# Attention scores as two full products and one split short one, and second-half copies on ScalarE in every unit

## The reference

```
sc = einsum('bhqd,bhkd->bhqk', q_blk, k).astype(float32) * scale
p  = softmax(sc, axis=-1)
o  = einsum('bhqk,bhkd->bhqd', p, v)
```

## Time and profile before

| what | us |
| --- | --- |
| median of 3 runs | 2406.16 (2404.14 to 2409.37) |
| profiled execution, its own time | 2408.83 |
| span of the profiled execution | 2407.0 |
| first attention stage | about 188 to 408 |
| second attention stage | about 1019 to 1238 |

### The profile page before, as it was taken

The page is one execution under the profiler, slowest core; times in us unless marked ns, Lnnn a source line. Parts: engine busy times, 40 slices in busy tenths (PEclk is TensorE's granted clock), DMA queues, the critical chain, the costliest instruction groups (busy, mean ns, idle before and its releaser), DMA issues.

```text
span 2407.0 us, 32363 instructions
## 1 busy us (share of the span) xinstructions
PE 2334.2 (97%) x12937; PEld 1777.2 (74%) x12937; DVE 1314.7 (55%) x2232; ACT 943.4 (39%) x1689; POOL 409.5 (17%) x614
## 2 busy tenths in 40 slices
PE   7999999999999999999999999999989999999998
PEld 7887888888777898788878887778755554745554
DVE  5567777242214365577763322336678856447644
ACT  6345556131113243355551311141354548822231
POOL 0034220000000001333100000000148952401011
PEclk9999999999999999999999999999999999999999
DMA  6010001222113210100021222224101011200000
GB/s 220 31 53 1 1 1 37 63 53 53 37 43 140 72 71 31 53 1 2 1 71 27 53 53 53 62 105 150 36 1 45 1 45 45 101 22 27 27 18 35
DMA packets 106645, 116.92 MB, mean 49 GB/s; under 512 B 20832, under 2 KB 78912, under 8 KB 106496
## 3 DMA queue, kind: packets, MB, share of 16 engines
q1 hardware_dynamic: 106208, 113.81, 15.2%
q10 hardware_dynamic: 288, 1.05, 0.1%
HBM read 96.82 MB, written 16.84 MB: 47 GB/s over the span
## 4 chain that ended last, share of the span: by engine, by line
PE 90%; DVE 5%; ACT 2%; issue 1%; POOL 1%; DMA 0%; SPq 0%; DVEq 0%; ACTq 0%
PE PS L732 8%; PE PS L792 7%; PE PS L795 7%; PE PS L798 7%; PE PS L564 7%; PE PS L756 5%; PE PS L950 5%; PE PS L1204 4%; PE PS L845 2%; PE PS L1173 2%; PE PS L1151 2%; PE PS L838 2%; PE PS L841 2%; PE PS L842 2%; PE PS L617 1%; PE PS L619 1%
## 5 line engine op out<-in xcount | busy, mean ns | idle before, releaser
L795 PE MATMUL PS<-hLo,R2bR 128*128 128x512 f32 x768 | 299.0, 389 | 0.0
L792 PE MATMUL PS<-hHi,R2bR 128*128 128x512 f32 x752 | 293.3, 390 | 0.0
L798 PE MATMUL PS<-hHi,R2bR 128*128 128x512 f32 x752 | 292.7, 389 | 0.0
L2303 DVE TENSOR_TENSOR R2bR<-W,R2bR 128x1024 fp32r<-128x1024 f32 x48 | 57.5, 1222 | 267.3 <-ACT R2bR L1575 267.3
L1642 ACT ACTIVATE R3a<-PS,pT 128x512 f32<-128x512 f32 x64 | 42.3, 688 | 403.6 <-PE PS L798 403.5
L1591 ACT ACTIVATE R2b<-PS,negm 128x1024 f32<-128x1024 f32 x128 | 142.6, 1114 | 62.3 <-DVE negm L2282 62.2
L950 PE MATMUL PS<-hT,W 128*128 128x512 f32 x384 | 166.0, 593 | 0.7 <-ACT R L1742 0.7
L795 PEld LDWEIGHTS PS<-hLo,R2bR 128*128 128x128 f32 x768 | 144.3, 188 | 29.5
L2282 DVE TENSOR_REDUCE negm<-PS 128x1 f32<-128x1024 f32 x128 | 156.5, 1222 | 17.0 <-PE PS L732 16.3
L792 PEld LDWEIGHTS PS<-hHi,R2bR 128*128 128x128 f32 x752 | 141.4, 188 | 30.1 <-issue 0.5
L798 PEld LDWEIGHTS PS<-hHi,R2bR 128*128 128x128 f32 x752 | 141.3, 188 | 29.6
(11 more groups left out here) (495 smaller groups left out, 5314.3 us busy)
## 6 DMA issues: line engine op xcount, KB each, us to landing
W<-in_w_in SPq DMA_DIRECT2D x10, 2048.0 KB, 8.3
W<-in_w_in SPq DMA_DIRECT2D x33, 512.0 KB, 4.3
W<-in_w_out SPq DMA_DIRECT2D x6, 2048.0 KB, 7.8
xres<-R SPq DMA_DIRECT2D x2, 4096.0 KB, 15.3
R<-xres SPq DMA_DIRECT2D x2, 4096.0 KB, 18.4
W<-in_w_in SPq DMA_DIRECT2D x4, 1024.0 KB, 6.5
R3a<-rsums SPq DMA_DIRECT2D x16, 256.0 KB, 5.5
W<-in_w_attn_proj SPq DMA_DIRECT2D x16, 256.0 KB, 5.8
```

Of the source, the lines that this page charges most:

```text
L792: mm = pe.matmul(o, wHi[c % 2][:, k, :], hi, start=(k == 0), stop=False)
L795: mm = pe.matmul(o, wHi[c % 2][:, k, :], hLo[:, k, ns], start=False, stop=False)
L798: mm = pe.matmul(o, wLo[c % 2][:, k, :], hi, start=False, stop=(k == 7))
L2303: dve.tensor_tensor(wLo[c % 2], w, wHi[c % 2].bitcast(F32), ALU.subtract).then_inc(s_wlo, 1)
```

## The change

For heads 1 to 7, the two halves of q and k are laid out anew. The 128 rows of a product now carry, besides the 64 + 32 rows of hi·hi, 32 rows of rope lo·hi; a second product of 128 rows carries nope hi·lo and lo·hi; the rope's hi·lo is left for a product of 32 rows. So a unit has four products of 128 rows and two of 32 rows, one for each half of the keys, whose rows lie in different 32-partition groups (`c_rows`). Head 0 keeps six products.

The rows are put in their places by 15 SBUF-to-SBUF transfers per head on SP's queue (`move_rows`), with waits on bank 7's free count and on the transfers' own semaphore between them, and TensorE waits for all 15 ahead of the head's first score product. The turns of k come at earlier units (`qk_steps`): for heads 2 to 7 at -1, +1, +2, +3 relative to the former head's first unit, and not -1, +1, +3, +5. ScalarE copies half 1 of the turned probabilities for every unit, VectorE half 0.

```diff
 def qk_steps(h):
-    return [1, 2, 3, 5] if h == 1 else [NT * (h - 1) + n for n in (-1, 1, 3, 5)]
+    return [1, 2, 3, 4] if h == 1 else [NT * (h - 1) + n for n in (-1, 1, 2, 3)]
...
+MOVES = 15
+def c_rows(h, n):
+    return slice(64 * (h % 2) + 32 * n, 64 * (h % 2) + 32 * n + 32)
...
-                    for n in range(2):
-                        for i, (x, y) in enumerate(((qh, kh), (qh, kl), (ql, kh))):
-                            mm = pe.matmul(PS[:, b + n, :], x[:, t * P:(t + 1) * P],
-                                           y[:, n * 512:(n + 1) * 512], start=(i == 0), stop=(i == 2))
+                    if h == 0:
...
+                    else:
+                        if t == 0:
+                            pe.wait_ge(s_moved, 16 * MOVES * (l * (H - 1) + h))
+                        for i, (x, y) in enumerate(((qh, kh), (ql, kl))):
+                            for n in range(2):
+                                pe.matmul(PS[:, b + n, :], x[:, ts_], y[:, n * 512:(n + 1) * 512],
+                                          start=(i == 0), stop=False)
+                        q_rope = qC[max(0, t // 2 - 1)]
+                        at_ = slice(t % 4 * P, (t % 4 + 1) * P) if t < 4 else slice(t % 2 * P, (t % 2 + 1) * P)
+                        for n in range(2):
+                            r = c_rows(h, n)
+                            mm = pe.matmul(PS[:, b + n, :], q_rope[r, at_], kC[r, :], start=False, stop=True)
...
+            def move_rows(l, h):
...
+                sp.wait_ge(free[7], bk.count(7))
+                move(qh[QK:P, :], ql[NOPE:QK, :]).then_inc(s_moved, 16)
+                for n in range(2):
+                    r = c_rows(h, n)
+                    move(qC[0][r, :], qh[NOPE:QK, 0:512]).then_inc(s_moved, 16)
+                    move(qC[1][r, :], qh[NOPE:QK, 512:768]).then_inc(s_moved, 16)
+                    move(qC[2][r, :], qh[NOPE:QK, 768:1024]).then_inc(s_moved, 16)
+                sp.wait_ge(s_moved, 16 * (moved + 7))
+                move(ql[NOPE:P, :], ql[0:NOPE, :]).then_inc(s_moved, 16)
+                sp.wait_ge(s_moved, 16 * (moved + 8))
+                move(ql[0:NOPE, :], qh[0:NOPE, :]).then_inc(s_moved, 16)
+                for n in range(2):
+                    ns = slice(512 * n, 512 * n + 512)
+                    bk.take(7)
+                    sp.wait_ge(free[7], bk.count(7))
+                    move(kh[QK:P, ns], kh[NOPE:QK, ns]).then_inc(s_moved, 16)
+                    move(kC[c_rows(h, n), :], kl[NOPE:QK, ns]).then_inc(s_moved, 16)
+                    sp.wait_ge(s_moved, 16 * (moved + 11 + 3 * n))
+                    move(kl[NOPE:P, ns], kh[0:NOPE, ns]).then_inc(s_moved, 16)
...
                     if u >= 1:
                         bk.take(4)
-                        if u % 2 == 0:
-                            o = arrive(5)
-                            act.activation(PT[1][:, 512:1024], o, ACT.Copy).then_inc(free[5], 1)
-                        else:
-                            bk.take(5)
+                        o = arrive(5)
+                        act.activation(PT[(u - 1) % 2][:, 512:1024], o, ACT.Copy).then_inc(free[5], 1)
...
-                        if u % 2 == 1:
-                            arrive(5)
-                            bk.take(4)
-                            dve.tensor_copy(PT[0][:, 0:512], PS[:, 4, :]).then_inc(free[4], 1)
-                            dve.tensor_copy(PT[0][:, 512:1024], PS[:, 5, :]).then_inc(free[5], 1)
-                        else:
-                            bk.take(5)
-                            o = arrive(4)
-                            dve.tensor_copy(PT[1][:, 0:512], o).then_inc(free[4], 1)
+                        bk.take(5)
+                        o = arrive(4)
+                        dve.tensor_copy(PT[(u - 1) % 2][:, 0:512], o).then_inc(free[4], 1)
```

More of the change, by code:

```diff
@@ L197, in build @@
         dft_d = sb("dft_d", [P, 2 * P])
-        u_mid = sb("u_mid", [P, FG, P])
+        u_mid, kC = sb2("u_mid", "k_rope_rest", [P, FG * P])
+        u_mid = u_mid[:, :].rearrange("p (g c) -> p g c", g=FG)
         with nc.sbuf_tensor("signs", [P, S], mybir.dt.int8) as signs:
@@ L250, in build @@
         qkT_lo = [[qk_lo[:, i, :], qk_lo[:, 2 + i, :]] for i in range(2)]
+        qC = [x.rearrange("p a b c -> p (a b c)") for x in (rtR[:, :, :, :],)] + [WR[:, i, 4096:4352] for i in range(2)]
         oT = R2a
@@ L328, in build @@
         scr = r3b[:, 1088:1088 + 40 * NPAIR].rearrange("p (i q) -> p i q", i=40)
-        CT = flat(u_mid).rearrange("p (i q c) -> p i q c", i=2, q=NPAIR)
+        CT = u_mid.rearrange("p g c -> p (g c)").rearrange("p (i q c) -> p i q c", i=2, q=NPAIR)
         Bb = rt[:, :, :, :].rearrange("p a b c -> p (a b c)").rearrange("p (i q c) -> p i q c", i=2, q=NPAIR)
@@ L423, in build @@
         s_qkT = sem("qkT_rounded")
+        s_moved = sem("qk_rows_moved")
         s_nm = sem("neg_max_ready")
@@ L729, in scores @@
                     (qh, kh), (ql, kl) = qkT[h % 2], qkT_lo[h % 2]
-                    for n in range(2):
-                        for i, (x, y) in enumerate(((qh, kh), (qh, kl), (ql, kh))):
-                            mm = pe.matmul(PS[:, b + n, :], x[:, t * P:(t + 1) * P],
-                                           y[:, n * 512:(n + 1) * 512], start=(i == 0), stop=(i == 2))
+                    ts_ = slice(t * P, (t + 1) * P)
+                    if h == 0:
+                        for n in range(2):
+                            for i, (x, y) in enumerate(((qh, kh), (qh, kl), (ql, kh))):
+                                mm = pe.matmul(PS[:, b + n, :], x[:, ts_],
+                                               y[:, n * 512:(n + 1) * 512], start=(i == 0), stop=(i == 2))
+                    else:
[10 more added lines that the diff above has]
+                            mm = pe.matmul(PS[:, b + n, :], q_rope[r, at_], kC[r, :], start=False, stop=True)
                     mm.then_inc(full[b], 1)
@@ L1315, in chunk, with move @@
                     load(k512, a["w_out"][l, :, n0:n0 + 512].rearrange("(k p) c -> p k c", p=P))
+            bk = Banks(full, free)
+            def move(dst, src):
+                return sp.dma_start(dst.bitcast(F32), src.bitcast(F32))
+            def move_rows(l, h):
+                (qh, kh), (ql, kl) = qkT[h % 2], qkT_lo[h % 2]
+                moved = MOVES * (l * (H - 1) + h - 1)
+                bk.take(7)
+                bk.take(7)
+                sp.wait_ge(free[7], bk.count(7))
[9 more added lines that the diff above has]
+                move(ql[0:NOPE, :], qh[0:NOPE, :]).then_inc(s_moved, 16)
+                for n in range(2):
+                    ns = slice(512 * n, 512 * n + 512)
+                    bk.take(7)
+                    sp.wait_ge(free[7], bk.count(7))
[3 more added lines that the diff above has]
+                    move(kl[NOPE:P, ns], kh[0:NOPE, ns]).then_inc(s_moved, 16)
             sp.wait_ge(s_init, 3)
@@ L1332, in _ @@
                     chunk(l, i)
+                for n in ROUND[:7]:
+                    bk.skip(n)
+                bk.take(turn_bank(0, 3))
+                for h in range(1, H):
+                    move_rows(l, h)
+                for b, n in enumerate(FIXED):
+                    bk.n[b] += n - (4 * (H - 1) + 1 if b == 7 else 0)
+                for n in ROUND[7:]:
+                    bk.skip(n)
                 sp.wait_ge(s_o, l + 1)
```

## The result

The changed kernel takes 2475.2 us (median of 4, 2472.2 to 2479.4), the kernel before 2405.5: a ratio of 1.0284, with a 95% interval of 1.0268 to 1.0301, 70 us slower. The forecast was slower by 18, in a range that ended at 2462. The profiled execution has a span of 2470.4.

A forecast was written before the change was run, and what follows sets the result against it. TensorE was taken to bound the kernel, with ScalarE's chain deciding from even to odd turn after the change. Per layer 4 us for pairs plus 4.9 at head 1, 2 × (4 + 4.9) = 18 us: 2424, range 2409 to 2462.

The forecast's parts named there:

- 8 on the pairs: Attention stages: pairs of units, with q/k turns and the last pair, make each layer about 4 us slower.
- 9.8 on the wait and clock at head 1: Head 1, each layer: TensorE waits 3.3 us for late moves and loses 1.6 to its clock, 4.9 together.
- 2.64 instead of 2.46: Even unit's turn to odd unit's turn: ScalarE's copy, then exp, decides at 2.64 us; TensorE's stream there was 2.46.
- I take 1.42: Score products ahead of P·V, heads 1 to 7: 1.42 us instead of 1.55, bounds 1.32 and 1.53.
- The one out is already in the 1.55: Ahead of P·V, the old 1.55 us already holds the change of form out, so only 0.10 is added.
- the 0.10 of the earlier trace: Second block's indexer: last group of short products to first full-height product takes 0.33 us, 0.10 more than a step.
- Eight are on the path: 2.4: Eight q or k turns per layer stand ahead of even units' turns, on the path, at 0.30 us each: 2.4.
- 15.6 is hidden by 0.4, which is no cover to speak of: Heads 2 to 7: the moves' chain takes 15.6 us (bounds 13.9 to 19.0), the time available is 16.0.
- the moves are late at every head: Rival, chance 0.20: heads 2 to 7 lose up to 2.8 us each, head 1 8.3 per layer; up to 2471.
- I charge the same: 1.6: Head 1, each layer: TensorE's clock after the wait costs 1.6 us, as after the idle time at the stage's begin.

The follow-up runs named there:

- the short chain: The changed kernel with the same 15 moves, the six of q's rope rows taken out of the chain of waits: 2444.4 us, ratio 1.0154.
- the filler: 26 small identity products ahead of TensorE's wait at head 1, added to the short chain: 2440.8 us, ratio 1.0143.

## Why the prediction was wrong

The direction and most mechanisms held; the time left the range by 13 us. Of the 18 us I had put 8 on the pairs and 9.8 on the wait and clock at head 1; measured, what lies outside the moves is 25.1 and the moves are 44.6. The step that failed is the length of the chain of moves against its cover. By the steps as they were put:

- **"2.64 instead of 2.46".** Right: 2.65, and the copies alone make the kernel slower by 20. The other half of the pair, from the odd turn on, I had left as it was; there the turn that has waited takes 0.72 and not 0.68, and the rest of it is in the next point. A pair is 6.80 where I had 6.63, some 4.5 a layer over 27 pairs, and the ends of the stage add 0.7: the first pair was 7.15, the last 7.02.
- **"I take 1.42"** for the score products ahead of P·V. Too low; 1.53 was my upper bound, and it was met. "The one out is already in the 1.55" is what was wrong: from a full product to P·V the kernel before takes 0.32, from the short pair it takes 0.43. The way out of the short form costs 0.20 over a step, not the 0.10 of the earlier trace rows, where groups of four short products were followed by a full one. The Trainium skill, TensorEngine Tiling (Array Packing), Key Properties, says that changing the tiling mode drains TensorE; the runs agree with that, at 0.21 us a unit more than one full step.
- **"Eight are on the path: 2.4".** Right for the turns (pairs of 7.14 beside 6.80, 2.4 a layer by the stages without the rounding), but one step was missing: behind the turn at unit 50 stands ScalarE's rounding of h. I followed TensorE's order past the moved turn and not ScalarE's. It costs 5.3 in both layers together, by the stages 4.8.
- **"15.6 is hidden by 0.4, which is no cover to speak of".** This is the step that failed. The chain of moves measured 17.2 to 19.5. Issues followed mostly at 0.62, where I took 0.45 between two rows although the SBUF-to-SBUF row had 0.60; over ten issues that is 1.5 us. The shift of 256 KB within SBUF landed in 2.9 and not 2.3. That makes 17.7; the shortest chains took 17.2 to 17.6, and those above had a slow issue or landing on top, for which my 15.6 had nothing. The cover was a little more than I had, 16.8 and not 16.0, and 12.9 and not 12.1 at head 1, as the pairs were longer. So the moves were late at six of the seven heads of each layer: by 0.5 to 2.9, and at head 1 by 5.8 to 6.4 instead of 3.5. My rival "the moves are late at every head" came true but for head 7, with a chance of 0.20, and 2475 lies above its price of up to 2471.
- **"I charge the same: 1.6"** for the clock at head 1. Too low: behind the long waits the two pairs at head 1 lost 3.7 and 4.7, and I had nothing for the other heads. The moves cost 27.4 us in the first stage and 15.1 in the second (against the kernel without them), of which 16.1 and 10.1 are waits; the remaining 16 us lie in the pairs behind the waits. Of these, 8.4 are at head 1, 5.9 at heads 2 to 4 of the first stage (1.5, 2.9 and 1.5, behind waits of 2.50, 2.86 and 2.63), and 1.5 at unit 50 there; behind the waits of 0.5 to 1.5 a head lost 0.1. At head 1 of the short chain the filler shows that this is the clock; for the other heads it is read from the granted clock alone.

By the experiments, from the kernel before on: ScalarE's copies +20.0 (by the stages 15.0, as said above); the short products beside them 17.3 - 20.0 = -2.7 (by the stages -1.7; with the old copies +4.8); the turn units beside both +7.8, of which 5.3 is the rounding; the moves 69.7 - 25.1 = +44.6. What stays open is why a single issue or landing in some chains took up to 1.7 us longer than the same one in others, and the few us outside the stages.

The thing that was meant to pay never did: a saved step is worth 19 us as a full product less, and as two short ones side by side it is worth -4.8.

## What to carry to other kernels

Replacing a full-height product by short ones side by side saves a step and pays two changes of form; here, with one pair per unit, they cost about as much as the product and a little more. Whether a longer run of short products between two changes would pay was not measured. Transfers that wait for one another have to be counted by their links, at the price of the nearest row of the same kind of memory, and a cover thinner than the spread of those rows is no cover. When a step is moved in one engine's order, go through the orders of all engines that have an instruction for it, and look at what stands behind it there.

## What the hardware showed that I had not expected

- Behind TensorE's waits for moves of 2.5 to 2.9 us in the changed kernel, the granted clock of the next 6 us was 0.58 to 0.72, and behind those of 5.8 and 6.4 it was 0.50 (two full products in 0.99 in place of 0.54). Behind waits of 0.5 to 1.0 it was 1.00 in every run. Between the two the same wait could go either way: 1.65 left it at 1.00 and 1.46 was followed by 0.58 in the changed kernel with the old copies.
- Two short products of 32 rows and 512 columns, in different row groups, count 0.33 from the last full one and 0.43 to P·V's 64-column form, and 0.44 to a full-height turn, where a full product's step is 0.23 and a full product counts 0.32 to P·V.
- A transposing-size product of 128 columns with the identity on both sides took 0.112 each in a row of 96 with the clock at 1.00, where the turns' products follow one another at 0.086 and I had reckoned with 0.057.
- Issues of SBUF-to-SBUF transfers follow one another at 0.62 on SP's queue, and at 0.55 behind the first one after a wait; single ones took 1.3 to 1.5.
